# Neighbourhood attention in column blocks of eight, in a one-core transformer kernel

## The chip, the cores and the metric

The kernel runs on one core of a Trainium2 chip, in one launch. The metric is the device time of the whole program in microseconds. It computes two transformer blocks one after the other on 1024 tokens of 1024 channels, all in float32.

## The reference

Only the first block holds neighbourhood attention. 1024 tokens lie on a grid of 16 rows by 64 columns; a query sees 8 rows by 16 columns of keys, clamped inside the grid, with a learned bias over the offset. There are 8 heads of 64 channels.

```python
def neighbourhood_attention(q, k, v, rpb):
    B, S, H, Dh = q.shape
    rows = S // GRID_W
    kh = min(NA_ROWS, rows)
    kw = NA_COLS
    qg = q.reshape(B, rows, GRID_W, H, Dh)
    kg = k.reshape(B, rows, GRID_W, H, Dh)
    vg = v.reshape(B, rows, GRID_W, H, Dh)
    cols = jnp.arange(GRID_W)
    col_start = jnp.clip(cols - kw // 2, 0, GRID_W - kw)
    col_idx = col_start[:, None] + jnp.arange(kw)[None, :]
    col_bias_idx = col_idx - cols[:, None] + (NA_COLS - 1)
    scale = Dh ** -0.5

    def row_block(r):
        row_start = jnp.clip(r - kh // 2, 0, rows - kh)
        q_r = lax.dynamic_index_in_dim(qg, r, axis=1, keepdims=False)
        k_rows = lax.dynamic_slice_in_dim(kg, row_start, kh, axis=1)
        v_rows = lax.dynamic_slice_in_dim(vg, row_start, kh, axis=1)
        k_win = k_rows[:, :, col_idx]
        v_win = v_rows[:, :, col_idx]
        s = jnp.einsum("bqhd,brqchd->bhqrc", q_r, k_win,
                       preferred_element_type=jnp.float32) * scale
        row_bias_idx = row_start + jnp.arange(kh) - r + (NA_ROWS - 1)
        bias = rpb[:, row_bias_idx][:, :, col_bias_idx]
        s = s + jnp.transpose(bias, (0, 2, 1, 3))[None].astype(jnp.float32)
        p = jax.nn.softmax(s, axis=(-2, -1))
        return jnp.einsum("bhqrc,brqchd->bqhd", p.astype(v_win.dtype), v_win)

    out = lax.map(row_block, jnp.arange(rows))
    return jnp.moveaxis(out, 0, 1).reshape(B, S, H * Dh)
```

What stands around it in the block (the second block follows, with another attention and another feed-forward part):

```python
    for l in range(DEPTH):
        h = rms_norm(x, norm1_g[l])
        z = h @ w_in[l]
        a, gate, q, k, v = jnp.split(z, splits, axis=-1)
        conv_out = conformer_conv(a, gate, dw_kernel[l], dw_bias[l],
                                  conv_ln_g[l], conv_ln_b[l])
        q = rms_norm(q.reshape(B, S, N_HEADS, HEAD_DIM), q_norm_g[l])
        k = rms_norm(k.reshape(B, S, N_HEADS, HEAD_DIM), k_norm_g[l])
        v = v.reshape(B, S, N_HEADS, HEAD_DIM)
        attn_out = neighbourhood_attention(q, k, v, rpb[l])
        mix = jnp.concatenate([conv_out, attn_out], axis=-1)
        x = x + mix @ w_out[l]
        h = rms_norm(x, norm2_g[l])
        x = x + (jax.nn.silu(h @ w_gate[l]) * (h @ w_up[l])) @ w_down[l]
```

## The kernel before

**Layout.** Activations lie by channels: a tile is 128 channels by 1024 tokens. A weight unit is 128 x 1024 numbers that SyncE loads (`load_unit`), GpSimd splits into a high and a low part (`split`, L339 and L341) and TensorE multiplies with the high and low parts of the activations in three products (`chunk`, L445), 48 matmuls of 512 columns. Each engine has a hand-written program; semaphores order them. Within an engine the instructions and their waits stand in the order in which they run.

**Ahead of the attention.** Units 0 to 7 give the gated input of the convolution. After each pair ScalarE takes a sigmoid (L916) and VectorE multiplies (L1257). ScalarE also issues the DMAs that build the bias tables in DRAM: 8 DMAs fill them with a masking value (L889), and `bias_windows` lays the bias in with 46 more, 16 large (L904) and 30 small (L911), between its second and third sigmoid. The depthwise convolution has 31 taps for each of 4 channel groups, 124 steps of VectorE (`conv`, L1236), which are spread between its other work.

**The attention.** It runs over four pairs of heads, c = 0 to 3. Each pair has three weight units (q, k, v; units 8 to 19 in all). VectorE evacuates each (L1273), ScalarE and VectorE normalise q and k by head and split them into high and low (`head_hi` L939, `head_lo` L1286). TensorE transposes v (L579) and ScalarE copies it (L955). Then 16 turns follow, n = 0 to 15: head n // 8, row pair n % 8. A turn has the 128 queries of two grid rows and the 8 or 9 key rows that they see (`key_rows`), so 512 or 576 keys of all 64 columns. Half of the turns have 9 rows. A turn goes so:

- TensorE `scores(n)` (L541): three products of q and k; 9 rows need a second matmul of 64 columns each. The result lies in one buffer of two PSUM banks, so `scores(n)` waits for `scores_max` of turn n - 1.
- VectorE adds the bias table and takes the row minimum of the negated sum (L1352). For 9 rows the bias is `bias_inner`, made at the start of each head (L1340 to L1343).
- ScalarE takes the exponential and its sum (L964).
- VectorE takes the reciprocal (L1293) and multiplies the probabilities by it (L1295).
- TensorE `turn(n)` (L556) transposes 4 or 5 blocks, ScalarE copies them (L848, called at L990 and L991), TensorE `values(n)` (L567) multiplies them with v.

TensorE's order is scores(n + 1), values(n - 1), turn(n). ScalarE's is exps(n + 1), the copy of n. VectorE's is bias and minimum of n, one convolution step (c < 3), reciprocal and multiply of n. In c = 3 the convolution is done. The layer norm of its output, its Silu (L977) and the split of the output projection's input (`mix_hi` on ScalarE, `mix_lo` L1264 on VectorE) stand between the turns instead. At the end of a pair ScalarE copies the output (L998).

SyncE loads the table of a head into `bias_table0` or `bias_table1` (L267), 2 DMAs a pair, once the head before is done with the buffer. `BD` in DRAM holds 16 rows of 64 keys for each of 128 queries of a head.

## Time and profile before

| | us |
|---|---|
| Median of 3 runs | 2851.19 |
| Lowest and highest run | 2848.6, 2851.89 |
| Span of the profiled execution | 2856.6 |
| TensorE busy, of the span | 2690.8 (94%) |
| VectorE busy | 1339.3 (47%) |
| ScalarE busy | 680.0 (24%) |
| GpSimd busy | 1009.8 (35%) |

PE is TensorE, DVE VectorE, ACT ScalarE, POOL GpSimd, SP SyncE; a "q" behind the name is the engine's queue, where DMAs are issued. A row of the timeline has the start, the length, the engine, the line, the operation with output and input, and in brackets how long the engine had been idle and what ended it. x8 joins eight instructions into one row. A row for a stretch gives its bounds and length, then for each engine the busy time and the number of instructions, and then the clock that TensorE was granted (1.00 is 2.4 GHz, 0.50 is 1.2 GHz), the DMA share and GB/s. A line number can be that of a helper.

### The profile page before, as it was taken

To read this page: it belongs to the slowest core of one execution; us is meant where nothing else is said; L and a number is where in the kernel's file an instruction comes from. 1 tells how busy PE (TensorE), PEld (TensorE's weight loads), DVE (VectorE), ACT (ScalarE), POOL (GpSimd) and SP (SyncE) were. 2 spreads that over 40 slices of the span, in tenths; PEclk is the share of its full clock that TensorE was granted. 3 is DMA by queue.
4 is the path that set the end of the run, shared out by engine and by line. 5 is a ranking of instruction groups with operands and counts; after the bars stand their busy time and mean duration, and the time that the engine had idled before them with its cause. 6 is when DMAs were issued, how large, how long until landed. Compare 5 with 4: busy or idle time off the path is not lost.

```text
span 2856.6 us, 29102 instructions
## 1 busy us (share of the span) xinstructions
PE 2690.8 (94%) x11492; PEld 2066.8 (72%) x11492; DVE 1339.3 (47%) x1449; ACT 680.0 (24%) x1016; POOL 1009.8 (35%) x554
## 2 busy tenths in 40 slices
PE   8798988899999999999989999997999999999979
PEld 6566766687888888887765665565788888888857
DVE  7768885424222222222755656755622222222465
ACT  3033444412000001000315445531300011100241
POOL 3311012043344444443533333324434343343353
PEclk9869998799999999999999999998999999999989
DMA  5200000121111111111100000001011111111112
GB/s 183 61 15 30 30 30 8 48 71 44 51 47 49 51 44 51 44 51 37 55 30 8 16 23 8 15 23 37 30 52 47 49 51 44 51 44 51 52 37 81
DMA packets 49351, 125.24 MB, mean 44 GB/s; under 512 B 19696, under 2 KB 19696, under 8 KB 48240
## 3 DMA queue, kind: packets, MB, share of 16 engines
q1 hardware_dynamic: 32400, 118.87, 12.6%
q10 hardware_dynamic: 16864, 5.18, 0.8%
q8 instruction: 59, 0.97, 0.1%
q14 instruction: 28, 0.23, 0.0%
HBM read 115.64 MB, written 9.37 MB: 44 GB/s over the span
## 4 chain that ended last, share of the span: by engine, by line
PE 77%; DVE 9%; issue 5%; ACT 3%; POOL 2%; ACTq 2%; DMA 1%; SPq 0%; POOLq 0%; DVEq 0%
PE ps L445 63%; PE ps L567 3%; PE ps L541 2%; PE ps L774 2%; DVE conv_out L1236 2%; PE ps L760 2%; PE ps L744 2%; PE ps L556 1%; PE ps L468 1%; ACTq L904 1%; POOL weight_hi L339 1%; DVE sb_softplus_lo L1533 1%; ACTq L911 1%; POOL weight_lo L341 1%; POOL branch_out L402 1%
## 5 line engine op out<-in xcount | busy, mean ns | idle before, releaser
L339 POOL TENSOR_TENSOR weight_hi<-weight_raw,zero_col 128x1024 fp32r<-128x1024 f32 (+1 forms) x195 | 373.2, 1914 | 1595.9 <-PE ps L445 1486.8
L445 PE MATMUL ps<-input_hi,weight_hi 128*128 128x512 f32 x2048 | 650.4, 399 | 52.9 <-DVE input_lo L1203 35.4
L445 PE MATMUL ps<-input_lo,weight_hi 128*128 128x512 f32 x2176 | 679.2, 394 | 18.5 <-DVE gate_lo L1603 16.7
L445 PE MATMUL ps<-input_hi,weight_lo 128*128 128x512 f32 x2048 | 634.0, 391 | 0.0
L341 POOL TENSOR_TENSOR weight_lo<-weight_raw,weight_hi 128x1024 fp32r<-128x1024 f32 (+1 forms) x195 | 497.3, 2550 | 15.3
L445 PEld LDWEIGHTS ps<-input_hi,weight_hi 128*128 128x128 f32 x2048 | 384.5, 190 | 161.6 <-issue 59.4
L445 PEld LDWEIGHTS ps<-input_lo,weight_hi 128*128 128x128 f32 x2176 | 413.3, 190 | 109.6 <-ACT input_lo L848 13.8
L445 PEld LDWEIGHTS ps<-input_hi,weight_lo 128*128 128x128 f32 x2048 | 387.2, 189 | 81.7
L445 PE MATMUL ps<-hidden_hi,weight_hi 128*128 128x512 f32 x864 | 232.0, 390 | 3.4 <-DVE hidden_lo L1418 3.4
L445 PE MATMUL ps<-hidden_lo,weight_hi 128*128 128x512 f32 x864 | 231.8, 390 | 0.0
L445 PE MATMUL ps<-hidden_hi,weight_lo 128*128 128x512 f32 x864 | 231.8, 390 | 0.0
L445 PEld LDWEIGHTS ps<-hidden_hi,weight_hi 128*128 128x128 f32 x864 | 162.8, 189 | 37.6 <-issue 3.8
L445 PEld LDWEIGHTS ps<-hidden_hi,weight_lo 128*128 128x128 f32 x864 | 162.8, 188 | 33.9
L445 PEld LDWEIGHTS ps<-hidden_lo,weight_hi 128*128 128x128 f32 x864 | 162.8, 188 | 33.9
L1236 DVE SCALAR_TENSOR_TENSOR conv_out<-glu_padded,taps_sb,conv_out 128x1024 f32<-128x1024 f32 x120 | 171.5, 1429 | 2.3
L1024 ACT ACTIVATE work_b<-work_a 128x1024 f32<-128x1024 f32 x32 | 34.0, 1062 | 563.9 <-DVE work_a L1413 563.9
L1427 DVE TENSOR_TENSOR branch_out<-ps,branch_out 128x1024 f32<-128x1024 f32 x56 | 65.9, 1219 | 204.8 <-PE ps L445 204.8
L1427 DVE TENSOR_TENSOR residual<-ps,residual 128x1024 f32<-128x1024 f32 x48 | 56.5, 1218 | 156.1 <-PE ps L445 156.1
L1413 DVE SCALAR_TENSOR_TENSOR work_a<-ps,token_scale 128x1024 f32<-128x1024 f32 x32 | 39.2, 1224 | 177.0 <-PE ps L445 168.0
L1405 DVE TENSOR_TENSOR work_c<-ps,token_scale 128x1024 f32<-128x1024 f32 x22 | 26.9, 1224 | 203.0 <-PE ps L445 203.0
L567 PE MATMUL ps<-probs_t,v_tokens 128*64 128x128 f32 (+1 forms) x576 | 98.1, 320 | 19.4 <-ACT probs_t L848 18.9
L1022 ACT ACTIVATE work_b<-work_a 128x1024 f32<-128x1024 f32 x22 | 23.4, 1062 | 378.5 <-DVE work_a L1402 378.5
(228 smaller groups left out, 2926.1 us busy)
## 6 DMA issues: line engine op xcount, KB each, us to landing
weight_raw<-w_ff SPq DMA_DIRECT2D x40, 512.0 KB, 3.5
weight_raw<-w_mlp SPq DMA_DIRECT2D x32, 512.0 KB, 3.5
weight_raw<-w_mlpd SPq DMA_DIRECT2D x32, 512.0 KB, 3.5
weight_raw<-w_ffd SPq DMA_DIRECT2D x20, 512.0 KB, 3.6
weight_raw<-w_out SPq DMA_DIRECT2D x16, 512.0 KB, 3.5
weight_raw<-w_in SPq DMA_DIRECT2D x16, 512.0 KB, 3.5
residual<-x SPq DMA_DIRECT2D x7, 1024.0 KB, 10.2
weight_raw<-w_qkv SPq DMA_DIRECT2D x12, 512.0 KB, 3.6
```

The source lines that it names most:

```text
L339: pool_.tensor_tensor(WH[:, slot, 0:width], raw, ZERO[:].to_broadcast([P, width]), ALU.add).then_inc(s["w_hi"], 1)
L341: pool_.tensor_tensor(WL[:, slot, 0:width], raw, WH[:, slot, 0:width].bitcast(f32), ALU.subtract).then_inc(s["w_split"], 1)
L445: last = mm(PS[:, b + 2 * c + h, :], w[:, slot, k * n + P * c:k * n + P * (c + 1)], a[:, k, h * H2:(h + 1) * H2], start=(k == 0 and step = ...
L541: last = mm(PS[:, 2 + b, 0:w], q[lo:lo + DH, rp * P:(rp + 1) * P], k_[lo:lo + DH, ks * GRID_W + b * 512:ks * GRID_W + b * 512 + w], start= ...
L567: last = mm(PS[DH * h:DH * (h + 1), 6 + rp // 4, (rp % 4) * P:(rp % 4 + 1) * P], V[0:w, ks // 2 + b, DH * h:DH * (h + 1)], PT[n % 2][0:w, ...
L744: last = mm(PS[:, n % 4, lo:], k_[r:r + DH, b * P:(b + 1) * P], q[r:r + DH, half * H2 + lo:(half + 1) * H2], start=(step == 0), stop=(step ...
L760: mm(PS[:, n % 4, lo:], NONE[:], RUN[n % 2][:, lo:], start=False, stop=False, skip_group_check=True)
L774: mm(PS[DH * h:DH * (h + 1), 6 + half, lo:], V2[:, b, DH * h:DH * (h + 1)], AW[n % 2][:, lo:], start=(b == 4 * half + 3), stop=(b == 0), s ...
L1024: act_.activation(TB[:], TA[:], ACT.Square).then_inc(s["ff_silu"], 1)
L1236: ins = stt(Y[:, c, :], src, TP[:, c, t:t + 1], Y[:, c, :], ALU.mult, ALU.add)
L1413: stt(TA[:], bank(b), 0.0, RS[:], ALU.max, ALU.mult).then_inc(s["bank_free"], 1)
L1427: ins = tt(dst, src, dst, ALU.add)
```

## The change

The queries are tiled by columns. Tokens are stored in 8 column blocks of 8 columns by 16 rows, 128 tokens each (`by_block`, `by_row` are the two views of one tile). A turn has the 128 queries of one block and all 16 rows of the blocks beside it: 3 key blocks, or 2 at the two edges (`key_blocks`). The rows outside the 8 of a query are masked by the bias table. Turns alternate between the two heads (`na_turn`). Scores fit one PSUM bank and there are two buffers of them, and two of the transposed probabilities in PSUM; in SBUF there are three of the scores. TensorE's order becomes scores(n + 2), values(n - 1), turn(n). The multiply by the reciprocal moves from VectorE to ScalarE, ahead of the next exponential. VectorE's order becomes bias and minimum of n + 1, reciprocal of n, the step beside it.

q and k (high and low), v at its evacuation and the output are written from one order into the other, in runs of 8 columns. The DRAM table is 64 x 7 x 120 numbers: one DMA masks it, 55 lay the bias in. GpSimd fills four SBUF tables with the masking value, and SyncE loads each head's table with 16 DMAs of 8 partitions, 32 a pair, 128 in all.

```diff
-def key_rows(rp):
-    first = [min(max(r - NA_ROWS // 2, 0), ROWS - NA_ROWS) for r in (2 * rp, 2 * rp + 1)]
-    return first[0], first[1] + NA_ROWS - first[0]
+CBLOCKS, CBW = 8, 8
+QB = ROWS * CBW
+N_KB = 7
+def na_turn(n):
+    return n % 2, n // 2
+def key_blocks(j):
+    first, last = max(j - 1, 0), min(j + 1, CBLOCKS - 1)
+    return first, last + 1 - first, 3 if j == 0 else 5 if j == CBLOCKS - 1 else 0
+def by_block(t):
+    return t.rearrange("p (b r c) -> p r b c", b=CBLOCKS, c=CBW)
+def by_row(t):
+    return t.rearrange("p (r b c) -> p r b c", b=CBLOCKS, c=CBW)
...
-        BT = [at(f"bias_table{i}", [P, 16, GRID_W], U4 + 4096 * i) for i in range(2)]
-        BI = at("bias_inner", [P, 9, GRID_W], U4 + 8192)
-        SB = [at(f"scores{i}", [P, 9 * GRID_W], U4 + 8192 + 2304 * (i + 1)) for i in range(2)]
-        ST = at("softmax_stats", [P, 3, 16], U4 + 8192 + 3 * 2304)
+        BT = [at(f"bias_table{i}", [P, N_KB, QB], U4 + 4 * N_KB * QB * i) for i in range(4)]
         OC = [at(f"attn_out{c}", [P, T], up32(c * UW)) for c in range(4)]
         QH, QL, KH, KL = (at(n, [P, T], QK0 + 4096 * i, f32r)
                           for i, n in enumerate(("q_hi", "q_lo", "k_hi", "k_lo")))
         V = at("v_tokens", [P, 8, P], QK0 + 16384)
-        PT = [at(f"probs_t{i}", [P, 5, P], QK0 + 20480 + 2560 * i) for i in range(2)]
+        PT = [at(f"probs_t{i}", [P, 3, P], QK0 + 20480 + 1536 * i) for i in range(2)]
+        SB = [at(f"scores{i}", [P, 3 * QB], QK0 + 23552 + 1536 * i) for i in range(3)]
+        ST = at("softmax_stats", [P, 3, 16], QK0 + 28160)
...
-        BD = nc.dram_tensor("bias_tables", [HEADS, P, 16 * GRID_W], f32).ap()
-        N_TABLE_DMAS = 2 * (HEADS + NA_COLS - 1)
+        BD = nc.dram_tensor("bias_rows", [HEADS * CBW, N_KB, (2 * NA_ROWS - 1) * CBW], f32).ap()
+        N_TABLE_DMAS = N_KB * CBW - 1
...
-                for h in (2 * c, 2 * c + 1):
-                    if h >= 2:
-                        sp.wait_ge(s["scores_max"], 8 * (h - 1))
-                    sp.wait_ge(s["scale_ready"], 1)
+                if c == 0:
+                    sp.wait_ge(s["bt_masked"], 4)
                     sp.wait_ge(s["table_out"], 16 * N_TABLE_DMAS)
-                    sp.dma_start(BT[h % 2][:], BD[h]).then_inc(s[f"bt_in{h % 2}"], 16)
+                elif c >= 2:
+                    sp.wait_ge(s["scores_max"], 16 * (c - 1))
+                for i in range(2):
+                    h, buf = 2 * c + i, 2 * (c % 2) + i
+                    for r in range(ROWS):
+                        first = min(max(r - NA_ROWS // 2, 0), ROWS - NA_ROWS)
+                        b0 = first - r + NA_ROWS - 1
+                        sp.dma_start(BT[buf][r * CBW:(r + 1) * CBW, :, first * CBW:(first + NA_ROWS) * CBW],
+                                     BD[h * CBW:(h + 1) * CBW, :, b0 * CBW:(b0 + NA_ROWS) * CBW])\
+                            .then_inc(s[f"bt_in{buf}"], 16)
...
-            splits(2, U_TAIL + 2 * TAIL - 2)
+            splits(2, 2)
+            pool.wait_ge(s["scale_ready"], 1)
+            for i in range(4):
+                pool_.memset(BT[i][:], MASKED).then_inc(s["bt_masked"], 1)
+            splits(4, U_TAIL + 2 * TAIL - 4)
...
-                    h, rp = n // 8, n % 8
-                    ks, nk = key_rows(rp)
+                    h, j = na_turn(n)
+                    kb, nb, _ = key_blocks(j)
                     lo = DH * h
                     if n == 0:
                         pe.wait_ge(s["qk_hi"], 2 * c + 2)
                         pe.wait_ge(s["qk_lo"], 2 * c + 2)
-                    else:
-                        pe.wait_ge(s["scores_max"], 16 * c + n)
+                    elif n >= 2:
+                        pe.wait_ge(s["scores_max"], 16 * c + n - 1)
                     for q, k_, step in ((QH, KH, 0), (QH, KL, 1), (QL, KH, 2)):
-                        for b, w in ((0, 512), (1, nk * GRID_W - 512)):
-                            if w:
-                                last = mm(PS[:, 2 + b, 0:w], q[lo:lo + DH, rp * P:(rp + 1) * P],
-                                          k_[lo:lo + DH, ks * GRID_W + b * 512:ks * GRID_W + b * 512 + w],
-                                          start=(step == 0), stop=(step == 2))
+                        last = mm(PS[:, 2 + n % 2, 0:nb * QB], q[lo:lo + DH, j * QB:(j + 1) * QB],
+                                  k_[lo:lo + DH, kb * QB:(kb + nb) * QB],
+                                  start=(step == 0), stop=(step == 2))
                     last.then_inc(s["scores_done"], 1)
                 def turn(n):
-                    _, nk = key_rows(n % 8)
                     pe.wait_ge(s["probs_scaled"], 16 * c + n + 1)
-                    if n:
-                        pe.wait_ge(s["pt_sb"], 16 * c + n)
-                    else:
+                    if n >= 2:
+                        pe.wait_ge(s["pt_sb"], 16 * c + n - 1)
+                    elif n == 0:
                         pe.wait_ge(s["v_ready"], c + 1)
-                    for b in range(5 if nk == 9 else 4):
-                        w = P if b < 4 else GRID_W
-                        last = nc.tensor.transpose(PS[0:w, 4 + b // 4, (b % 4) * P:(b % 4 + 1) * P],
-                                                   SB[n % 2][:, b * P:b * P + w], IDENT[:])
+                    for b in range(key_blocks(na_turn(n)[1])[1]):
+                        last = nc.tensor.transpose(PS[:, 4 + n % 2, b * P:(b + 1) * P],
+                                                   SB[n % 3][:, b * QB:(b + 1) * QB], IDENT[:])
                     last.then_inc(s["pt_done"], 1)
                 def values(n):
-                    h, rp = n // 8, n % 8
-                    ks, nk = key_rows(rp)
+                    h, j = na_turn(n)
+                    kb, nb, _ = key_blocks(j)
                     pe.wait_ge(s["pt_sb"], 16 * c + n + 1)
-                    nb = 5 if nk == 9 else 4
                     for b in range(nb):
-                        w = P if b < 4 else GRID_W
-                        last = mm(PS[DH * h:DH * (h + 1), 6 + rp // 4, (rp % 4) * P:(rp % 4 + 1) * P],
-                                  V[0:w, ks // 2 + b, DH * h:DH * (h + 1)], PT[n % 2][0:w, b, :],
+                        last = mm(PS[DH * h:DH * (h + 1), 6 + j // 4, (j % 4) * P:(j % 4 + 1) * P],
+                                  V[:, kb + b, DH * h:DH * (h + 1)], PT[n % 2][:, b, :],
                                   start=(b == 0), stop=(b == nb - 1), skip_group_check=True)
                     last.then_inc(s["pv_done"], 1)
...
+                scores(1)
                 for n in range(16):
-                    if n < 15:
-                        scores(n + 1)
+                    if n < 14:
+                        scores(n + 2)
...
-            for h in range(HEADS):
-                act.dma_start(BD[h], NEG[:]).then_inc(s["neg_out"], 16)
+            act.dma_start(BD.rearrange("q k b -> q (k b)"), NEG[0:HEADS * CBW, 0:N_KB * 15 * CBW]).then_inc(s["neg_out"], 16)
             def bias_windows():
-                act.wait_ge(s["neg_out"], 16 * HEADS)
+                act.wait_ge(s["neg_out"], 16)
                 rows, cols = 2 * NA_ROWS - 1, 2 * NA_COLS - 1
+                per = N_KB * rows * CBW
+                def window(q, block, x0, x1, bias_col):
+                    dst = bass.AP(tensor=BD.tensor, offset=q * per + block * rows * CBW + x0,
+                                  ap=[[CBW * per, HEADS], [CBW, rows], [1, x1 - x0]])
+                    src = bass.AP(tensor=rpb.tensor, offset=bias_col,
+                                  ap=[[rows * cols, HEADS], [cols, rows], [1, x1 - x0]])
+                    act.dma_start(dst, src).then_inc(s["table_out"], 16)
                 half = NA_COLS // 2
-                inner = GRID_W - NA_COLS + 1
-                with nc.allow_non_contiguous_dma(reason="64-byte windows of the bias"):
...
+                with nc.allow_non_contiguous_dma(reason="windows of the bias, 32 bytes at most"):
+                    for q in range(CBW):
+                        window(q, 0, q, CBW, half - 1)
+                        window(q, 1, 0, CBW, 2 * half - 1 - q)
+                        if q:
+                            window(q, 2, 0, q, 3 * half - 1 - q)
+                        for k in range(2):
+                            window(q, 3 + k, 0, CBW, NA_COLS - 1 - q + CBW * k)
+                            window(q, 5 + k, 0, CBW, half - 1 - q + CBW * k)
...
-                    copy((QH, KH)[j][:], (TA, TB)[j][:]).then_inc(s["qk_hi"], 1)
+                    copy(by_block((QH, KH)[j][:]), by_row((TA, TB)[j][:])).then_inc(s["qk_hi"], 1)
...
+                    act.wait_ge(s["probs_sum"], 16 * c + n + 1)
+                    act_.activation(SB[n % 3][:, 0:w], SB[n % 3][:, 0:w], ACT.Identity,
+                                    scale=ST[:, 2, n:n + 1]).then_inc(s["probs_scaled"], 1)
...
-                copy(OC[c][:], bank(6)).then_inc(s["attn_out_done"], 1)
-            act.wait_ge(s["attn_out_done"], 4)
+                for half in range(2):
+                    copy(by_row(OC[c][:]).rearrange("p r b c -> p b r c")[:, 4 * half:4 * half + 4],
+                         PS[:, 6 + half, :].rearrange("p (b r c) -> p b r c", b=4, c=CBW))\
+                        .then_inc(s["attn_out_done"], 1)
...
-                    tt(t[:], bank(2 * ((u + j) % 2)), RS[:], ALU.mult).then_inc(s["bank_free"], 1)
+                    if j < 2:
+                        tt(t[:], bank(2 * ((u + j) % 2)), RS[:], ALU.mult).then_inc(s["bank_free"], 1)
+                    else:
+                        tt(by_block(t[:]), by_row(bank(2 * ((u + j) % 2))), by_row(RS[:]), ALU.mult)\
+                            .then_inc(s["bank_free"], 1)
...
-                    tt((QL, KL)[j][:], (TA, TB)[j][:], (QH, KH)[j][:].bitcast(f32), ALU.subtract)\
-                        .then_inc(s["qk_lo"], 1)
+                    tt(by_block((QL, KL)[j][:]), by_row((TA, TB)[j][:]), by_block((QH, KH)[j][:].bitcast(f32)),
+                       ALU.subtract).then_inc(s["qk_lo"], 1)
+                def scores_in(m):
+                    h, j = na_turn(m)
+                    _, nb, at_bias = key_blocks(j)
+                    w, buf = nb * QB, 2 * (c % 2) + h
+                    if j == 0:
+                        dve.wait_ge(s[f"bt_in{buf}"], 16 * ROWS * (c // 2 + 1))
+                    dve.wait_ge(s["scores_done"], 16 * c + m + 1)
+                    if m >= 3:
+                        dve.wait_ge(s["pt_done"], 16 * c + m - 2)
+                    dve_.tensor_tensor_reduce(
+                        out=SB[m % 3][:, 0:w], in0=PS[:, 2 + m % 2, 0:w],
+                        in1=BT[buf][:, at_bias:at_bias + nb, :].rearrange("p b k -> p (b k)"),
+                        scale=-1.0, scalar=3.0e38, op0=ALU.add, op1=ALU.min,
+                        accum_out=ST[:, 0, m:m + 1]).then_inc(s["scores_max"], 1)
                 def probs(m):
-                    w = key_rows(m % 8)[1] * GRID_W
                     dve.wait_ge(s["probs_done"], 16 * c + m + 1)
-                    chain(dve_.reciprocal(ST[:, 2, m:m + 1], ST[:, 1, m:m + 1]))
-                    chain.wait()
-                    ts(SB[m % 2][:, 0:w], SB[m % 2][:, 0:w], ST[:, 2, m:m + 1], None, ALU.mult)\
-                        .then_inc(s["probs_scaled"], 1)
+                    dve_.reciprocal(ST[:, 2, m:m + 1], ST[:, 1, m:m + 1]).then_inc(s["probs_sum"], 1)
                 if c == 3:
@@ -1330,29 +1382,11 @@
                 dve.wait_ge(s["qk_scaled"], 2 * c + 2)
                 head_lo(1)
                 evac(2, TC)
+                scores_in(0)
                 for n in range(16):
...
-                        chain(dve_.tensor_copy(BI[:], BT[h % 2][:, 3:12, :]))
-                        chain(dve_.memset(BI[0:GRID_W, 8, :], MASKED))
-                        chain(dve_.memset(BI[GRID_W:P, 0, :], MASKED))
...
+                    if n < 15:
+                        scores_in(n + 1)
+                    probs(n)
```

## Rows read from the trace of the kernel before

**Rows 1.** Stretches, the turn loops of c=0, 1, 3; last: clock, DMA share, GB/s.
```profile
167.60:236.20 68.60, 66.20 (x297) 47.52 (x297) 46.95 (x89) 24.98 (x57) 1.00 (x1) 0.68 0.07 24
...
279.70:332.30 52.60, 48.86 (x297) 35.42 (x297) 47.29 (x89) 24.72 (x57) 3.15 (x2) 0.97 0.09 31
...
475.30:558.30 83.00, 67.89 (x301) 47.36 (x301) 38.59 (x84) 43.32 (x76) 0.00 (x0) 0.73 0.00 0
```

**Rows 2.** Timeline: start, length (us), engine, line; VectorE in a turn of c=1.
```profile
300.17 0.69 DVE L1352 CUSTOM_DVE_ANT_0 scores<-ps,bias_table 128x512 f32<-128x512 f32 x1 [0.24 <-PE ps L541]
...
300.79 1.28 DVE L1236 SCALAR_TENSOR_TENSOR conv_out<-glu_padded,taps_sb,conv_out 128x1024 f32<-128x1024 f32 x1
...
302.10 0.16 DVE L1293 RECIPROCAL softmax_stats<-softmax_stats 128x1 f32<-128x1 f32 x1
...
302.30 0.48 DVE L1295 TENSOR_SCALAR scores<-scores,softmax_stats 128x512 f32<-128x512 f32 x1
...
303.16 0.69 DVE L1352 CUSTOM_DVE_ANT_0 scores<-ps,bias_table 128x512 f32<-128x512 f32 x1 [0.37 <-PE ps L541]
```

**Rows 3.** Timeline, TensorE in two turns of 8 key rows of c=0.
```profile
207.13 0.79 PE L541 MATMUL ps<-k_hi,q_hi 64*128 64x512 f32 x1
...
208.70 1.97 PE L567 MATMUL ps<-probs_t,v_tokens 128*64 128x128 f32 x8
...
210.60 1.12 PE L556 MATMUL ps<-identity,scores 128*128 128x128 f32 x4
211.65 0.50 PE L541 MATMUL ps<-k_hi,q_hi 64*128 64x512 f32 x1
...
214.14 0.50 PE L541 MATMUL ps<-k_hi,q_hi 64*128 64x512 f32 x1
```

**Rows 4.** Timeline, TensorE at the start of two turns of 9 key rows, c=0.
```profile
184.99 0.85 PE L541 MATMUL ps<-k_hi,q_hi 64*128 64x512 f32 x2
...
190.82 0.79 PE L541 MATMUL ps<-k_hi,q_hi 64*128 64x512 f32 x1
```

**Rows 5.** A stretch of 3 us in turns of 9 key rows, c=0.
```profile
197.00:200.00 3.00, 3.00 (x11) 2.04 (x10) 1.67 (x3) 1.32 (x4) 0.00 (x0) 0.50 0.00 0
```

**Rows 6.** Groups by form, 160 to 560 us: busy us, mean ns, idle before.
```profile
L848 ACT ACTIVATE probs_t<-ps 128x512 f32<-128x512 f32 x64 | 37.4, 584 | 20.7 <-PE ps L556 20.7
...
L1352 DVE CUSTOM_DVE_ANT_0 scores<-ps,bias_inner 128x576 f32<-128x576 f32 x32 | 24.2, 755 | 17.8 <-PE ps L541 17.0
...
L964 ACT ACTIVATE scores<-scores,softmax_stats 128x512 f32<-128x512 f32 x32 | 23.1, 721 | 38.7 <-DVE softmax_stats L1352 38.7
```

**Rows 7.** Timeline, ScalarE and VectorE late in c=3.
```profile
529.15 4.63 ACT L977 ACTIVATE conv_out<-conv_out,gains_sb 128x1024 f32<-128x1024 f32 x4
...
552.32 1.23 DVE L1264 TENSOR_TENSOR input_lo<-attn_out,input_hi 128x1024 fp32r<-128x1024 f32 x1 [1.83 <-ACT input_hi L848]
```

**Rows 8.** Timeline ahead of the loops; line L911 alone (ns: least, median, most).
```profile
39.08 9.02 ACTq L889 DMA_DIRECT2D bias_tables<-masked_tile  x8
...
L911 ACTq DMA_DIRECT2D bias_tables<-rpb x30: 648/648/3467, 67.3 to 104.9; - x30
...
94.01 11.49 ACTq L911 DMA_DIRECT2D bias_tables<-rpb  x15
...
105.55 1.06 ACT L916 ACTIVATE work_b<-work_a 128x1024 f32<-128x1024 f32 x1 [51.12 <-issue]
...
106.72 2.37 DVE L1257 TENSOR_TENSOR glu_padded<-work_c,work_b 128x1024 f32<-128x1024 f32 x1 [14.93 <-ACT work_b L916]
...
137.90 3.78 PE L468 MATMUL ps<-squares,mean_head 128*128 128x512 f32 x4 [19.39 <-ACT squares L932]
```

**Rows 9.** Line L267 alone; ScalarE's timeline: a table load, a later identity.
```profile
L267 SPq DMA_DIRECT2D bias_table<-bias_tables x8: 326/326/377, 107.1 to 422.9; - x8
...
535.59 1.28 ACT L964 ACT_TABLE_LOAD   x1
...
646.83 2.19 ACT L873 ACTIVATE input_hi<-residual,gains_sb 128x1024 fp32r<-128x1024 f32 x2 [8.56 <-PE ps L445]
```

55 lines of the change are left out of this document (11 added, 44 removed).

## The prediction

> **What bounds the kernel now.** I read the page first, then the chain of waits, then the stretches, then single turns in the timeline. The page's chain puts most of the span on matmuls of the weight units, which the change leaves alone; what it touches lies between 42 us and 581 us. There the same pattern comes four times, once for each pair of heads c: three weight units (q, k, v), and then 16 attention turns. The stretches [rows 1] give the turns' length: 68.6 us for c=0, 52.6 for c=1 (c=2 is the same, 52.5), 83.0 for c=3, together 256.7 us. The reader should see the granted clock beside them: 0.68 and 0.73 in the long ones, 0.97 in the short ones.
>
> At c=1 and c=2 one turn takes VectorE 2.99 us (the scores of one turn at 300.17, of the next at 303.16), of which 0.37 us is waiting for the scores from TensorE [rows 2]. So VectorE and TensorE bound it together, since there is one score buffer. At c=0 TensorE bounds it alone: at half clock a turn of 8 key rows takes it 4.52 us (207.13 to 211.65), at full clock 2.49 us (211.65 to 214.14) [rows 3], and a turn of 9 key rows at half clock 5.83 us (184.99 to 190.82) [rows 4]. The stretch 197 to 200 shows TensorE busy all of the time, at a clock of 0.50 [rows 5]. Being busy did not bring the clock back there.
>
> **A turn after the change.** 12 of the 16 turns of a pair have three key blocks (384 columns), 4 have two (256), in place of 512 or 576.
>
> VectorE: the bias-and-minimum goes from 512 to 384 columns. Its slope, from 689 and 755 ns at 512 and 576 [rows 2, 6], is 1.03 ns a column, so it holds the engine 0.62 - 0.13 = 0.49 us. The convolution step stays (1.31 us from start to start), the reciprocal too (0.20), and the multiply at L1295 (0.49 us) goes [rows 2]. Sum 2.00 us, 1.87 with two blocks; 16 turns are 31.5 us. The copy of `bias_inner` and its memsets go as well; they are part of the 52.6 us.
>
> ScalarE takes the multiply over. Exp costs 721 ns at 512 columns and the copy of the transposed probabilities 584 [rows 6]; at 384 columns, with some 0.12 us of overlap, I take 0.5 for exp, 0.19 for reading its sum, 0.5 for the new scaling, 0.45 for the copy: 1.7 us. That hides beside VectorE's 2.0 and beside TensorE, and costs nothing while either is slower.
>
> TensorE: at half clock, the 8-row turn splits into scores 1.57 us, values 1.90, transposes 1.05 [rows 3]. Two 512-column scores start 0.43 us apart there, so 128 columns are 0.107 us, and three score matmuls of 384 take 1.57 - 3 x 0.107 = 1.25. Values and transposes go from four blocks to three: 1.43 and 0.79. Sum **3.47 us**; with two blocks 2.41. Sixteen turns are 51.3 us. At full clock the same shares of 2.49 us give 1.9 us, just under VectorE's 2.00. So the clock decides: 2.0 or 3.5 us a turn. With a start of some 5 us and a tail of 1 to 2 us, a pair costs 37 us or 54 us.
>
> **Which clock.** I compare how much of a turn is columns streaming, at 0.107 us for 128 columns and twice that for each matmul of a value or transpose block (8 and 4 of them in an 8-row turn). The 8-row turn then streams 3 x 0.43 + 12 x 0.213 = 3.84 us of its 4.52, or 0.85; the 9-row turn (64 columns more, 15 matmuls) 4.64 of 5.83, or 0.80. At 0.50 clock the 9-row turns stayed at half clock; in both long stretches the clock rose within 8-row turns. The new turn (3 x 0.32 + 9 x 0.213) streams 2.88 us of 3.47, or 0.83, and with its small overheads taken in full (3.56 us) 0.81. That is nearer to the turns that did not recover. And the start of each pair, where TensorE waits for q, k and the first softmax, is unchanged, and the clock was at half at the start of all four loops, for about 3 us at c=1 and c=2. So I take half clock for most of each loop.
>
> The Trainium skill, "TensorE: Matmul & The Clock Gate", section "Why this matters for your kernels", advises to keep TensorE busy without a break to reach full clock. The stretch with busy 3.00 of 3.00 at 0.50 [rows 5] disagrees. By the page's rule the new loops would all run fast; that is the rival below.
>
> **The four loops, at half clock.** Three scores lie ahead of the first transposes (0.93 + 0.93 + 1.25 = 3.1 us), so what follows the start is 51.3 - 3.1 = 48.2.
> - c=0: start 5.3 (6.1 before; exp and scale now have two blocks), 48.2, tail 1.0: 54.5 for 68.6, gain 14.
> - c=1, c=2: 4.5 (5.1 before) + 48.2 + 1.0, less 2 for turns that still run at full clock: 51.7 for 52.6, gain 1 each. What VectorE saves there is not on the path, since TensorE is late instead. The next unit needs no convolution that isn't done.
> - c=3: layer norm and output split lie between the turns. Up to its first transposes 8.2 (7.4 before, and one score more); the first three turns, of which two carry a table load, Ln and Exp of the layer norm on ScalarE (2.6 each), 10.3; seven turns at 3.47, 24.3; the turn in which four Silus hold ScalarE for 4.63 us [rows 7], with their table load and a copy 7.0, 10.5; one turn with the table load of 1.28 us, 4.1; four turns 12.5; tail 1.5. Sum 71.4 for 83.0, gain 11.6. In its last turns the bound was a ring of waits: VectorE waited 1.83 us for ScalarE's copy [rows 7] before it took the reciprocal. The new order takes the reciprocal first and opens the ring; next late is TensorE (3.47) or ScalarE (1.7 and its copy of 1.0).
>
> **In front of the loops.** ScalarE issues the bias tables' DMAs from 54.4 to 105.5 us, and the sigmoid behind them waits 51.12 us; VectorE waits 14.93 us for that sigmoid; at 137.90 TensorE has been idle 19.39 us [rows 8]. So this queue sets the end here. Eight writes of the mask table become one (9.02 us of issue from 39.08 on [rows 8], less one of 1.2), so the first sigmoid comes before VectorE needs it, and the windows start about 3 us earlier. 46 windows become 55, all of the small kind at L911, median 648 ns, at worst 3467 [rows 8]. One group of 15 took 11.49 us, 0.77 each [rows 8], and behind the large windows others took up to 0.87. At 0.65 the 55 end at 87, at 0.87 at 99. VectorE can't be at the sigmoid's result before 89. Gain 6 to 17, taken **12**, all on the path: unit 8's result was there at 118.5 (137.90 less 19.39), some 17 us before VectorE came for it, so up to 17 us nothing else is late.
>
> Moved past SP: 128 table loads of 56 pieces each take the place of 8. One load held SP 0.33 us [rows 9]; 32 at 0.33 to 1.6 us are 10 to 52 us, from 99 at the latest, and the first scores need them at about 155 (167.6 less 12). The loads for c=1 to c=3 and the weights behind them have the length of a loop. Cost 0; from 1.8 us a load on the scores would wait, and a load with 0.33 is far from it. GpSimd fills four tables ahead of its split of unit 4; TensorE is then at work on units 2 and 3 (11 us each), and the split waits for that: cost 0, at worst a few us.
>
> **Layout.** q, k (high and low), v and the output are written in chunks of 8 columns: about 6.8 us a pair of 1.0 to 1.2 us instructions. The trace shows none with such chunks. The nearest rows are the same instructions without chunks, so I take no difference; doubled they would cost 27 us in all. Less than nothing is excluded: no element falls away.
>
> Sum: 12 + 14 + 1 + 1 + 11.6 = **40 us**. The profiled execution spans 2856.6, the median of the runs is 2851.2, so 5 less: 2817 in a profile, **2811** in the runs.
>
> **The rivals.**
> 1. *Full clock in one or both of c=1 and c=2.* These two regained it in 3 us before (0.97 in their rows). Then each gains 16 instead of 1 (start and tail 5, and 31.5, for 52.6). Time 2796 or 2781. Against it: the new turn's share. Chance 0.22.
> 2. *Full clock everywhere.* c=0 gains 30, c=3 25: 12 + 30 + 16 + 16 + 25 = 99 us, 2752. For it: TensorE no longer waits within a turn. Chance 0.15.
> 3. *Chunked layout or slow table loads* take 15 to 40 us back: 2826 to 2851. Chance 0.08.
> 4. *Slower: the new scaling needs another function table than exp.* Then each turn loads twice, 2 x 1.28 = 2.57 us, on ScalarE: 1.7 + 2.6 = 4.3 us a turn, 275 us in 64 turns, with starts and c=3's extras 308 for 256.7. Less 12 in front: 2890. It decides from a turn of 3.7 us on. Against it: the same function ran at 646.83 under the table that was loaded for exp at 535.59, with no load between [rows 9]. Chance 0.05, with other losses of that size in it. The Trainium skill, "ScalarE: Activation LUTs", section "Table sets: the hidden batching unit", says that identity is in every set; rows 9 agree.
>
> My forecast has the other 0.50; its own range, from the front's bounds and 3.47 or 3.56 a turn, is 2800 to 2825.
>
> **Numbers.** A difference under 0.2% (6 us) can't be told from none. Faster: 0.50 + 0.22 + 0.15 + most of 0.08 = 0.93; same 0.02; slower 0.05. The range takes in rival 2 and half of rival 3: 2748 to 2836.
>
> **What would show it.** In the new profile: scores, values and transposes at 3.5 us a turn with a clock near 0.5 in the four loops, or 2.0 us with 1.0; VectorE's turn without L1295; the sigmoid's wait near 38 us; TensorE's 19.4 us gap near 7; no table loads beyond the present ones; the loops at 54, 52, 52 and 71 us. Wrong it is if the clock rises in three-block turns, or if a strided write takes more than 1.3 us.

## The result and the profile after

| | before | after |
|---|---|---|
| Median of the runs | 2849.89 us (4 runs, 2848.35 to 2851.89) | 2831.70 us (4 runs, 2830.00 to 2833.28) |
| Span of the profiled execution | 2856.6 us | 2828.3 us |
| VectorE busy | 1339.3 us | 1288.7 us |
| ScalarE busy | 680.0 us | 682.7 us |
| GpSimd busy | 1009.8 us | 1014.6 us |

The ratio is 0.9933, with a 95% interval from 0.9919 to 0.9948. The change makes the kernel faster by 18.2 us, where the forecast said 40. The sign was right and the time lies in the range, but the gain is less than half of the forecast one.

The stretches of the changed kernel, from the first score of each loop of turns to its last value, and what lies between them. After the bounds and the length come the busy times of TensorE, its weight load, VectorE, ScalarE and GpSimd, then the granted clock. They answer to [rows 1].

```profile
156.56:213.53 56.97, 54.37 (x189) 37.25 (x189) 32.57 (x67) 25.38 (x65) 2.92 (x2) 0.50 0.06 15
213.53:259.25 45.72, 40.50 (x153) 30.69 (x153) 36.53 (x34) 12.95 (x16) 10.60 (x5) 0.91 0.12 30
259.25:313.36 54.11, 50.84 (x189) 34.81 (x189) 32.58 (x67) 25.41 (x65) 3.02 (x2) 0.56 0.05 13
313.36:358.70 45.34, 40.13 (x153) 30.25 (x153) 37.80 (x35) 12.95 (x16) 10.60 (x5) 0.92 0.12 30
358.70:413.15 54.45, 51.19 (x189) 35.13 (x189) 32.58 (x67) 25.41 (x65) 3.01 (x2) 0.56 0.05 13
413.15:461.56 48.41, 39.83 (x158) 30.16 (x157) 29.70 (x27) 17.18 (x20) 14.54 (x6) 0.92 0.04 11
461.56:527.28 65.72, 56.44 (x193) 37.62 (x193) 25.48 (x62) 44.05 (x84) 0.00 (x0) 0.53 0.00 1
```

The reader should see the clock column. All four loops run at half clock almost throughout, also those of c=1 and c=2, which had 0.97 in [rows 1]. The work of a turn shrank, VectorE fell from 47.3 to 32.6 us a loop, and the loops of c=1 and c=2 are still 1.5 and 2 us longer than they were.

One turn of c=0 on VectorE (start, length, engine, line, operation; in brackets the idle time before it and what ended it). It answers to [rows 2]:

```profile
173.43 0.56 DVE L1339 CUSTOM_DVE_ANT_0 scores<-ps,bias_table 128x384 f32<-128x384 f32 x1 [1.73 <-PE ps L571]
173.92 0.08 DVE L1339 DVE_READ_ACCUMULATOR2_ANT softmax_stats<- 128x1 f32 x1
173.92 0.16 DVE L1348 RECIPROCAL softmax_stats<-softmax_stats 128x1 f32<-128x1 f32 x1
173.99 1.26 DVE L1270 SCALAR_TENSOR_TENSOR conv_out<-glu_padded,taps_sb,conv_out 128x1024 f32<-128x1024 f32 x1
177.00 0.56 DVE L1339 CUSTOM_DVE_ANT_0 scores<-ps,bias_table 128x384 f32<-128x384 f32 x1 [1.74 <-PE ps L571]
```

The turn is 3.57 us here, of which VectorE waits 1.74 for TensorE. The multiply is gone.

In front of the loops: ScalarE's queue, its sigmoid, VectorE behind it, and TensorE's gap. They answer to [rows 8]:

```profile
51.82 38.19 ACTq L931 DMA_DIRECT2D bias_rows<-rpb  x55
90.06 1.06 ACT L946 ACTIVATE work_b<-work_a 128x1024 f32<-128x1024 f32 x1 [37.18 <-issue]
91.23 1.22 DVE L1291 TENSOR_TENSOR glu_padded<-work_c,work_b 128x1024 f32<-128x1024 f32 x1 [0.42 <-ACT work_b L946]
129.81 3.44 PE L500 MATMUL ps<-squares,mean_head 128*128 128x512 f32 x4 [9.93 <-ACT squares L962]
```

The 55 windows took 0.69 us each. The sigmoid waits 37.18 us for them instead of 51.12, VectorE 0.42 instead of 14.93, and TensorE's gap is 9.93 instead of 19.39. The loops start at 156.56 instead of 167.59 [rows 1].

### The profile page after: what moved, and what is told of

Its sections match the earlier page's. It is cut to its first block, busy times and chain, and to the rows that moved or that the text cites. A ratio compares the mean times of both kernels' runs of the same rounds, so it can differ in the third digit from the quotient of the medians.

```text
span 2828.3 us, 28250 instructions
## 1 busy us (share of the span) xinstructions
PE 2680.4 (95%) x11060; PEld 2053.4 (73%) x11060; DVE 1288.7 (46%) x1361; ACT 682.7 (24%) x1052; POOL 1014.6 (36%) x558
## 4 chain that ended last, share of the span: by engine, by line
PE 78%; DVE 10%; issue 5%; ACT 3%; POOL 2%; ACTq 1%; DMA 0%; SPq 0%; POOLq 0%; DVEq 0%
PE ps L477 64%; PE ps L593 3%; DVE conv_out L1270 2%; PE ps L571 2%; PE ps L802 2%; PE ps L584 2%; PE ps L788 2%; PE ps L772 2%; ACTq L931 1%; DVE sb_softplus_lo L1566 1%; PE ps L500 1%; POOL weight_hi L367 1%; POOL weight_lo L369 1%; POOL branch_out L434 1%; PE ps L792 1%
## 5 line engine op out<-in xcount | busy, mean ns | idle before, releaser
L477 PE MATMUL ps<-input_lo,weight_hi 128*128 128x512 f32 x2176 | 684.0, 396 | 19.1 <-DVE gate_lo L1636 17.3
L1270 DVE SCALAR_TENSOR_TENSOR conv_out<-glu_padded,taps_sb,conv_out 128x1024 f32<-128x1024 f32 x120 | 178.9, 1491 | 2.4
L593 PE MATMUL ps<-probs_t,v_tokens 128*64 128x128 f32 x352 | 90.7, 427 | 12.8 <-ACT probs_t L876 12.8
```

Source lines behind the costliest of these rows:

```text
L477: last = mm(PS[:, b + 2 * c + h, :], w[:, slot, k * n + P * c:k * n + P * (c + 1)], a[:, k, h * H2:(h + 1) * H2], start=(k == 0 and step = ...
L593: last = mm(PS[DH * h:DH * (h + 1), 6 + j // 4, (j % 4) * P:(j % 4 + 1) * P], V[:, kb + b, DH * h:DH * (h + 1)], PT[n % 2][:, b, :], start ...
L1270: ins = stt(Y[:, c, :], src, TP[:, c, t:t + 1], Y[:, c, :], ALU.mult, ALU.add)
```

## The experiments

**The theory.** At half clock the new turn takes TensorE 3.56 us, where a turn of 8 rows took 4.52 and one of 9 rows 5.83 [rows 3, 4], but the loops now stay at half clock, and that is where the gain stays. What decides is not how much of a turn is streaming, by which my forecast chose, but the entry of a loop: the clock is lost there, and the new turns neither lose nor regain it. **The rivals** are that the mix of matmuls within a turn decides the clock (the forecast's own reason), that something else than the clock bounds the new loops (the chunked layout, the tables, ScalarE), and that part of the missing gain is no loss at all but comes from the profile that the sum started from.

### The base of the sum

The kernel before was run again, unchanged, ten times.

> The kernel before, unchanged, timed and profiled again. Its profile before spanned 2856.6 us, while its four runs had a median of 2849.9; the profiled run of the changed kernel spans 2828.3 with a median of 2831.7. Theory A (the clock of the loop at c=0 differs from one execution to the next, and the profile of before was one where it rose late): the span here is 2845 to 2852 us, and the loop of c=0 is some 3 to 9 us shorter than 68.6 us, the other loops the same. Rival B (the profile adds its own cost to the kernel before): the span is again 2856 and the loop at c=0 68.6.

Measured: 2851.32 us, a ratio of 1.0003 (0.9993 to 1.0013), with runs from 2847.24 to 2857.80. This time the profiled execution spans 2846.6 us, 10.0 less than the one that the forecast read. Its stretches:

```profile
167.76:224.55 56.79, 54.27 (x297) 39.43 (x297) 46.77 (x89) 24.71 (x57) 1.03 (x1) 0.85 0.08 29
224.55:267.82 43.27, 38.05 (x153) 28.86 (x153) 36.62 (x35) 12.89 (x15) 10.60 (x5) 0.96 0.08 25
267.82:323.51 55.69, 52.73 (x297) 38.31 (x297) 47.38 (x89) 24.71 (x57) 3.11 (x2) 0.88 0.09 29
...
366.76:422.47 55.71, 52.69 (x297) 38.27 (x297) 47.39 (x89) 24.71 (x57) 3.12 (x2) 0.88 0.09 29
...
469.48:546.36 76.88, 64.52 (x301) 45.67 (x301) 38.67 (x84) 43.23 (x76) 0.00 (x0) 0.74 0.00 1
```

The same program gives c=0 56.8 us here and 68.6 in [rows 1], c=1 55.7 and 52.6, c=3 76.9 and 83.0. The start is the same (167.76 and 167.59). So in the kernel before each loop's length hangs on when the clock rises in it, and this differs from execution to execution. TensorE's transposes show when, at c=0:

```profile
178.90 1.12 PE L556 MATMUL ps<-identity,scores 128*128 128x128 f32 x4
183.90 1.14 PE L556 MATMUL ps<-identity,scores 128*128 128x128 f32 x5
187.47 0.77 PE L556 MATMUL ps<-identity,scores 128*128 128x128 f32 x5
```

The second row belongs to turn 2, the first with 9 rows. Its five transposes would take 1.33 us at half clock and take 0.77 at full, so the clock rose in the middle of them. At c=1 and c=2 it rose in turn 2 as well (five in 1.15 us at c=1), and at c=3 in turn 5, all of them turns of 9 rows. In the profile that the forecast read, the loop of c=0 stayed at half through all its 9-row turns of the first head and rose only behind them.

Against this execution the change gives 11.2 us in front, -0.2 at c=0, 1.6 and 1.3 at c=1 and c=2, 11.2 at c=3, and loses 5.9 in the three stretches between. The spans differ by 18.3 us, as the medians do (18.2). This is theory A, only wider: it had 3 to 9 us at c=0 and the other loops unchanged. Rival B, a cost of the profiling, falls, since this profiled run took 2848.53 us among runs of 2847.24 to 2857.80.

### Is it the clock?

Extra matmuls whose results nobody reads were put into the loops of the changed kernel: twelve ahead of turn 0, and four in each of turns 1 to 3 of c=0 to c=2.

```diff
+                def warm(b, count):
+                    for _ in range(count):
+                        mm(PS[:, b, :], QH[:, 0:P], KH[:, 0:512], start=True, stop=True)
...
                     if n < 14:
                         scores(n + 2)
+                    if n == 0:
+                        warm(5, 12)
+                    elif n < 4 and c < 3:
+                        warm(0, 4)
                     if n:
                         values(n - 1)
                     turn(n)
```

> The changed kernel with filler matmuls (128x512, into a bank that nobody reads): 12 ahead of the first transposes of each pair, 4 in each of turns 1 to 3 for c=0 to 2. Nothing else differs. Theory A (the clock decides the turn: 3.56 us at half, about 2.0 at full, where VectorE is the bound): the clock is up from the third turn on in c=0 to c=2 and stays up, each of these loops falls from 54 to 57 us to 38 to 41 us, and the run is 40 to 50 us faster than the changed kernel, near 2785 us. Rival B (the chain of waits from exp over reciprocal, scaling, transposes and copy bounds the turn too): the clock rises but a turn stays above 2.6 us, and the gain is under 25 us. Rival C (the clock falls again in the turns without fillers): gain under 10 us.

Measured: 2781.59 us (2781.00 to 2782.51), a ratio of 0.9748 (0.9732 to 0.9764), so more work gives 50 us less than the changed kernel, as theory A had it. The loops of c=0 to c=2 take 41.6, 38.65 and 38.64 us at clocks of 0.92, 1.00 and 1.00. VectorE in two turns of c=0:

```profile
178.92 1.27 DVE L1278 SCALAR_TENSOR_TENSOR conv_out<-glu_padded,taps_sb,conv_out 128x1024 f32<-128x1024 f32 x1
180.22 0.56 DVE L1347 CUSTOM_DVE_ANT_0 scores<-ps,bias_table 128x384 f32<-128x384 f32 x1
180.71 0.08 DVE L1347 DVE_READ_ACCUMULATOR2_ANT softmax_stats<- 128x1 f32 x1
180.84 0.17 DVE L1356 RECIPROCAL softmax_stats<-softmax_stats 128x1 f32<-128x1 f32 x1
180.92 1.27 DVE L1278 SCALAR_TENSOR_TENSOR conv_out<-glu_padded,taps_sb,conv_out 128x1024 f32<-128x1024 f32 x1
```

From one step to the next (178.92 to 180.92) it is 2.00 us, the forecast's number for full clock, and VectorE has no idle time left. The chunked layout, the tables and ScalarE are the same in this kernel, so the rival that one of them bounds the loops falls.

Then the extra matmuls were spread: c + 1 of them in every turn, and none at the entry beyond that.

> The changed kernel with fillers in every turn, of the same kind: 1 a turn at c=0, 2 at c=1, 3 at c=2, none at c=3. At half clock one costs TensorE 0.43 us. Theory A (how densely columns stream through a turn is what lets the clock rise or keeps it down): at c=0 the clock stays at half through the loop (turns of 4.0 us, loop near 62 us), at c=2 it rises and the loop is near 40 us, c=1 lies on one or the other side. Rival B (the clock is down because of the pauses at the start of the pair, not of the turns): all three stay at half, with turns of 4.0, 4.4 and 4.8 us.

Measured: 2814.74 us in one run.

```profile
158.68:223.22 64.54, 63.32 (x205) 40.74 (x205) 30.68 (x66) 25.36 (x65) 1.02 (x1) 0.53 0.05 12
267.45:309.97 42.52, 40.98 (x221) 26.20 (x221) 31.32 (x66) 25.48 (x65) 3.03 (x2) 1.00 0.07 17
353.56:399.25 45.69, 44.49 (x237) 29.19 (x237) 31.51 (x66) 25.39 (x65) 3.04 (x2) 1.00 0.06 16
```

One wide matmul in each turn left c=0 at half clock and cost 7.6 us there. Two and three a turn held full clock at c=1 and c=2, which come in at it. That is the pattern of theory A, but it doesn't show theory A, since two and three matmuls also shorten the wait ahead of turn 0. Against the 34.6 us that these loops reach further below, 8 and 11 us are the price of the matmuls themselves.

The same matmuls as in the first of these kernels, in the kernel before:

> The kernel before with the fillers of e1_warm_start: 12 ahead of the first transposes of each pair, 4 in each of turns 1 to 3 for c=0 to 2. Theory A (the clock was also what made the loop of c=0 long before, and c=1 and c=2 had it at full already): the loop at c=0 falls from 60 to 68 us to about 53, c=1 and c=2 stay within 2 us of 52.6, the run is 8 to 16 us faster than the kernel before, near 2837. Then the retiling itself, both at full clock, is worth about 50 us. Rival B: no change within 0.2%.

Measured: 2853.57 us (2851.41 to 2859.95), a ratio of 1.0002 (0.9991 to 1.0013). Two of its loops:

```profile
169.14:228.45 59.31, 57.81 (x321) 41.62 (x321) 46.77 (x89) 24.83 (x57) 1.03 (x1) 0.91 0.08 27
271.98:326.95 54.97, 53.33 (x321) 38.51 (x321) 47.43 (x89) 24.83 (x57) 3.13 (x2) 1.00 0.09 29
```

The clock rose here too, to 1.00 at c=1, and nothing was gained; the 8 to 16 us that theory A expected did not come. At full clock VectorE works on an old turn for all but 0.24 to 0.37 of its 2.99 us [rows 2], so an old loop at full clock has little left to gain from a faster TensorE. The clock is not worth nothing to them: c=0 took 68.6 us at 0.68 and 56.8 at 0.85. But they regain most of it by themselves, and the 24 extra matmuls of a loop cost about as much as they bring: c=1 takes 55.0 us at 1.00 with them and took 52.6 at 0.97 without. With the same extra matmuls in both kernels, the change is worth 72.0 us (2853.57 less 2781.59) in place of 18.2.

### Where the clock is lost

The entries of c=0 (first row) and of c=1 in the changed kernel, TensorE:

```profile
156.56 0.51 PE L571 MATMUL ps<-k_hi,q_hi 64*128 64x256 f32 x1 [2.16 <-DVE work_c L1310]
...
259.25 0.38 PE L571 MATMUL ps<-k_hi,q_hi 64*128 64x256 f32 x1 [1.32 <-DVE work_c L1310]
...
263.23 0.44 PE L584 MATMUL ps<-identity,scores 128*128 128x128 f32 x2 [1.61 <-ACT scores L1000]
...
265.46 0.44 PE L571 MATMUL ps<-k_hi,q_hi 64*128 64x384 f32 x1
265.74 0.37 PE L571 MATMUL ps<-k_lo,q_hi 64*128 64x384 f32 x1
265.91 0.52 PE L571 MATMUL ps<-k_hi,q_lo 64*128 64x384 f32 x1
266.36 1.11 PE L593 MATMUL ps<-probs_t,v_tokens 128*64 128x128 f32 x4
```

TensorE waits 1.61 us for the first softmax, does one turn at full clock, and is at half clock from about 265.8 on: the four value matmuls that took 0.65 us take 1.11. From 266 to 300 it is busy 34.00 of 34.00 us, and the clock is 0.50 all the time. At c=0 the loop comes in at half clock already: the clock was 1.00 until 156.5, and fell at the end of a wait of 2.16 us.

In the kernel before, the same happens at c=1:

```profile
284.79 0.66 PE L556 MATMUL ps<-identity,scores 128*128 128x128 f32 x4 [1.96 <-DVE scores L1295]
...
286.72 1.95 PE L567 MATMUL ps<-probs_t,v_tokens 128*64 128x128 f32 x8
```

Up to the 1.96 us wait and just behind it the clock is full (four transposes in 0.66 us), then the eight value matmuls take 1.95 us, as at half clock (1.97 in [rows 3]).

The next kernel has the twelve matmuls ahead of turn 0 of c=0 to c=2, which close this wait, and none in the turns.

```diff
                     if n < 14:
                         scores(n + 2)
+                    if n == 0 and c < 3:
+                        warm(5, 12)
                     if n:
                         values(n - 1)
                     turn(n)
```

> The changed kernel with the twelve extra 128x512 matmuls ahead of the first transposes of the turn loops of c=0 to c=2, and without the four in each of turns 1 to 3. (Their results are never read.) With both, the loops took 41.6, 38.7 and 38.6 us at a clock of 0.92, 1.00 and 1.00 and the kernel 2781.6 us. Theory A, the clock is settled by how TensorE enters the loop: the loops are 36 to 40 us each and the time is 2781.6 less three times twelve matmuls of 0.22 us, 2773 to 2779 us. Theory B, entering at full clock is not enough, since in the changed kernel the loops of c=1 and c=2 were entered at full clock and fell two or three turns in: the waits of turns 1 to 3 lose it again, c=1 and c=2 take 54 to 57 us each, c=0 40 to 60, and the time is 2815 to 2840 us.

Measured: 2769.71 us (2768.79 to 2772.21), ratio 0.9718 (0.9702 to 0.9734), 3 us below theory A's window of 2773 to 2779.

```profile
158.43:196.53 38.10, 36.50 (x201) 25.90 (x201) 31.29 (x66) 25.29 (x65) 1.02 (x1) 0.92 0.08 21
196.53:240.06 43.53, 38.31 (x153) 29.06 (x153) 38.59 (x35) 12.96 (x16) 10.60 (x5) 0.96 0.12 31
240.06:275.16 35.10, 33.50 (x200) 23.68 (x200) 31.13 (x66) 25.29 (x65) 3.04 (x2) 1.00 0.08 21
```

The turns are the changed kernel's own, and they hold full clock to the end of the loop. So their mix of matmuls does not lose it; the entry does. The wait of 1.32 us ahead of the first score of c=1 is still there (240.06), and the clock did not fall behind it alone. Whether it is the length of the second wait that counts, or both waits together, nothing here separates; closing the second is enough. The second row shows one thing more: the stretch behind the loop is 43.53 us instead of 45.72, since its first weight unit starts at full clock.

Five matmuls in place of the twelve:

> The kernel with extra matmuls ahead of turn 0 of c=0 to c=2, but five instead of twelve: 1.1 us at full clock, under the 1.61 us that TensorE waited there in c=1 of the changed kernel. Theory A, the wait ahead of turn 0 is what loses the clock, and most of it filled is enough at c=1 and c=2: their loops take 33.5 to 35 us; c=0, which comes in at half clock (12 filled 4.1 us and raised it), stays at 0.50 and 55 to 58 us: time 2782 to 2788 us. Theory B, the length of the run matters: all three loops fall back to 54 to 57 us, 2828 to 2835 us. Theory C, any filling will do: all three at 33 to 37 us, 2764 to 2769 us.

Measured: 2766.03 us (2765.79 to 2768.87), theory C. The loops take 36.39, 34.60 and 34.60 us at 0.91, 1.00 and 1.00. Even c=0, which comes in at half clock, rises with 2.4 us of wide matmuls. I had expected it to need more. The stretches behind the loops of c=0 and c=1 take 44.65 and 44.28 us, about 1 us more than with twelve. The trace shows where at c=0: TensorE waits 3.90 us for ScalarE in the middle of the stretch in both kernels, and the clock falls there in both, but with five it falls before the four 512-column matmuls behind the wait (3.78 us), with twelve during them (3.06 us).

Twenty narrow matmuls (128 columns each), with as many columns as five wide ones:

> The changed kernel with twenty extra matmuls of 128 columns ahead of turn 0 of c=0 to c=2, in place of the five or twelve of 512 columns: as many columns as five wide ones, 1.1 us of them at full clock, more with what each costs beside its columns. Theory A, what counts is that TensorE has no gap ahead of turn 0, whatever the matmuls: c=1 and c=2 keep full clock (34 to 37 us each), and c=0, which comes in at half, rises as with five wide ones (36 to 39 us): 2765 to 2775 us. Theory B, narrow matmuls close the gap but cannot raise the clock: c=1 and c=2 34 to 37 us, c=0 at 0.50 and 56 to 60 us: 2786 to 2794 us. Theory C, narrow ones neither hold nor raise it: all at 54 us or more, 2832 us or more.

Measured: 2791.22 us (2789.72 to 2793.34), theory B.

```profile
157.14:217.32 60.18, 58.65 (x209) 41.61 (x209) 32.58 (x67) 25.28 (x65) 1.03 (x1) 0.50 0.05 13
...
262.91:297.57 34.66, 33.06 (x209) 23.74 (x209) 30.85 (x66) 25.53 (x65) 3.03 (x2) 1.00 0.08 21
```

These two rows separate two things. A loop that comes in at full clock (c=1) keeps it as soon as the wait is closed, with matmuls of either width. A loop that comes in at half clock (c=0) stays there: narrow matmuls ran 4.53 us without a gap ahead of turn 0 and did not raise it, and the loop stays at 0.50 for all of its 60 us. Five wide ones did.

Five wide matmuls in turn 4, in the middle of the loop, where there is no wait to close, and none at the entry:

> The changed kernel with five extra matmuls of 512 columns in turn 4 of the loops of c=0 to c=2 only, where TensorE is busy without a gap at half clock; nothing ahead of turn 0. Theory A, a run of wide matmuls raises the clock anywhere and the turns then hold it: from turn 5 on turns of 2.00 us, the loops of c=0 to c=2 take 40 to 46 us each, the time is 2790 to 2805 us. Theory B, only the gap ahead of turn 0 counts, and once the loop runs at half clock it stays: the loops are as in the changed kernel plus five matmuls (2 us each), 2834 to 2842 us.

Measured: four runs of 2824.80, 2799.21, 2781.67 and 2800.24 us. The runs lie in steps of some 20 us. The profiled execution is the longest; its loops take 43.21, 58.21 and 56.89 us. At c=0 the clock rose:

```profile
174.99 2.50 PE L562 MATMUL ps<-k_hi,q_hi 128*128 128x512 f32 x5
177.42 1.32 PE L597 MATMUL ps<-probs_t,v_tokens 128*64 128x128 f32 x6
178.68 0.55 PE L588 MATMUL ps<-identity,scores 128*128 128x128 f32 x3
```

The transposes after it take 0.55 us for three, where they took 0.90, and the turns are 2.0 us to the end. At c=1 and c=2 the same five did not raise it. So wide matmuls can raise the clock in mid-loop, and the turns then hold it, but these five did so only once of three times in this execution, and by the step between the runs (18 to 25 us for each loop that rises) twice in two of the others and three times in the fourth. The granted clock of the runs, averaged over the whole program, steps the same way: 0.946 here, 0.956 in the runs of about 2800 us, 0.964 in that of 2781.67. In which loops it rose there was not seen. Neither theory had this.

### What the second score buffer is worth

TensorE's order goes back to that of the kernel before, so that only one score buffer is in use at a time; first without extra matmuls.

```diff
-                    elif n >= 2:
-                        pe.wait_ge(s["scores_max"], 16 * c + n - 1)
+                    else:
+                        pe.wait_ge(s["scores_max"], 16 * c + n)
...
-                scores(1)
                 for n in range(16):
-                    if n < 14:
-                        scores(n + 2)
+                    if n < 15:
+                        scores(n + 1)
```

> The changed kernel with that same older order of the scores and nothing else: one score buffer in use at a time, no extra matmuls. Theory A, at half clock TensorE has 2.4 us of transposes and value matmuls between the scores of one turn and those of the next, which hides VectorE's read: turns stay at 3.56 us, the loops within 1 us each and the time 2828 to 2836 us. Theory B, the second buffer carries the gain of the change: turns grow by 0.5 us or more, 2850 us or more.

Measured: 2845.35 us (2841.07 to 2847.59), between the two theories: 13.7 us slower than the changed kernel. Its loops take 59.3, 58.0, 57.4 and 69.1 us, 2.3 to 3.9 more each. A three-block turn at half clock is 3.64 us instead of 3.56, and turns 1 and 2 wait 0.34 and 0.43 us for ScalarE. Theory A had TensorE's own work as the bound, which it is, but not these small waits, which add up over 64 turns and four starts. At c=1 the clock falls sooner too: behind the wait of 1.80 us ahead of turn 0 TensorE is at half clock at once, where the changed kernel still does one turn at full clock.

The same order together with the twelve matmuls ahead of turn 0:

> The kernel with twelve extra matmuls ahead of turn 0 (2769.7 us, turns of 2.00 us at full clock), with the order of the kernel before: the scores of turn n+1 are issued in turn n and wait until VectorE has read those of turn n, so one score buffer is in use at a time. Theory A, the second buffer is what lets a full-clock turn run without a gap: the turn becomes 2.3 to 3.0 us, the loops of c=0 to c=2 take 40 to 48 us and the time is 2782 to 2808 us; if the gaps also lose the clock, up to 2825 us. Theory B, the second buffer hides nothing: within 3 us of 2769.7 us.

Measured: 2844.93 us (2843.58 to 2847.57), 75 us slower than with two buffers, and past the end of either theory. The entry of c=1, TensorE:

```profile
265.36 3.02 PE L562 MATMUL ps<-k_hi,q_hi 128*128 128x512 f32 x12
...
270.70 0.44 PE L588 MATMUL ps<-identity,scores 128*128 128x128 f32 x2 [0.80 <-ACT scores L1005]
...
273.33 0.90 PE L588 MATMUL ps<-identity,scores 128*128 128x128 f32 x3 [0.90 <-ACT scores L1005]
```

The loop enters at full clock, then TensorE waits 0.80 and 0.90 us for the scaled probabilities in turns 1 and 2, and the clock is at half from there on; the loops take 60.1, 57.4 and 57.4 us. So the second buffer is worth 14 us to the changed kernel. With the wait ahead of turn 0 closed, it decides whether there is a full clock at all: it takes away the two waits behind which the clock falls.

### Where the multiply stands

The scaling back on VectorE, behind the reciprocal, in the changed kernel:

```diff
-                    act.wait_ge(s["probs_sum"], 16 * c + n + 1)
-                    act_.activation(SB[n % 3][:, 0:w], SB[n % 3][:, 0:w], ACT.Identity,
-                                    scale=ST[:, 2, n:n + 1]).then_inc(s["probs_scaled"], 1)
...
-                    dve_.reciprocal(ST[:, 2, m:m + 1], ST[:, 1, m:m + 1]).then_inc(s["probs_sum"], 1)
+                    chain(dve_.reciprocal(ST[:, 2, m:m + 1], ST[:, 1, m:m + 1]))
+                    chain.wait()
+                    ts(SB[m % 3][:, 0:w], SB[m % 3][:, 0:w], ST[:, 2, m:m + 1], None, ALU.mult)\
+                        .then_inc(s["probs_scaled"], 1)
```

> The changed kernel with one part undone: the scaling of the probabilities is back on VectorE behind the reciprocal, and ScalarE's Identity is gone. In the changed kernel a turn takes 3.56 us at half clock and VectorE waits 1.74 us of it for TensorE. Theory A, TensorE at half clock hides either place: loops as in the changed kernel within 1 us, time 2828 to 2834 us. Theory B, the multiply behind the 1.27 us step of the convolution on VectorE lengthens the chain from scores to transposes past what the second score buffer covers: each turn grows by 0.3 us or more, time 2845 us or more.

Measured: 2828.92 us (2827.42 to 2830.06), theory A and 2.8 us less than the changed kernel. At c=3 ScalarE is busy 36.43 us instead of 44.05, and the loop takes 63.44 instead of 65.72. At half clock this part of the change brought nothing, and took some 2.3 us where ScalarE is loaded.

The same with the extra matmuls of the first kernel of this kind:

> The kernel with the extra matmuls at the start of each loop (2781.6 us), and the scaling of the probabilities moved from ScalarE back to VectorE behind the reciprocal. At full clock a three-block turn of c=0 to c=2 took 2.00 us with VectorE at work without a gap. Theory A, VectorE is the bound at full clock, as the forecast had it (2.00 us a turn): the multiply on 384 columns, some 0.5 us by the 0.755 us that it took on 576, comes on top, the loops of c=0 to c=2 grow from 38.6 to 43 to 47 us and the time is 2795 to 2808 us. Theory B, TensorE is the bound at 1.99 us and VectorE only keeps step: VectorE has room elsewhere, the loops grow by under 2 us each and the time is 2781 to 2788 us.

Measured: 2787.15 us (2785.76 to 2789.49), 5.6 more than with the multiply on ScalarE. That is theory B's window, and the loops grew by under 2 us, as theory B had it. But its reason does not hold: VectorE has no idle time in a turn that went from 2.00 to 2.33 us (one step at 179.46, the next at 181.78), so VectorE sets its length. The loops of c=1 and c=2 grew from 38.65 to 40.3 only, because without the move the four extra matmuls make each of turns 1 to 3 some 2.9 to 3.1 us long and leave VectorE slack there. The stretches behind c=0 and c=1 grew as well, from 43.5 to 45.3 and 45.2, and c=3 is 2.6 us shorter: 1.7 + 1.6 + 1.7 + 1.8 + 1.6 - 2.6 = 5.8, beside 5.6 between the times. So theory A has the right bound, and its sum is too large; the move gains only at full clock.

### The loop of c=3

Four extra matmuls in every turn of c=3 beside those of the first such kernel:

> The kernel with twelve extra matmuls ahead of turn 0 and four in turns 1 to 3, and in the loop of c=3 four extra matmuls of 128x512 in every turn from 1 to 15, into the bank that the turn's own transposes will overwrite. Before, that loop took 67.6 us at a clock of 0.58. Theory A, the clock bounds that loop too: it rises to 0.95 or more, the loop becomes ScalarE's (44 us busy, with its Silu stall of some 4 us) and takes 50 to 57 us, the kernel 2765 to 2772 us, the fastest so far. Theory B, that loop waits for its own side work on ScalarE and VectorE whatever the clock: the clock rises, the loop stays at 62 us or more, the kernel at 2776 to 2784 us.

Measured: 2774.97 us (2771.76 to 2777.97), between the theories. The loop took 63.06 us at a clock of 0.90. Its middle turns are 3.12 us instead of 2.00, since the extra matmuls are on the path there. So only the gaps were filled, where TensorE waits for ScalarE's table loads (9 and 10 matmuls, turns 2 and 3) and for its Silu (25, turn 11), with twelve ahead of turn 0 and none in the other turns:

> The kernel with twelve extra matmuls ahead of turn 0 in the loops of c=0 to c=2 (2769.7 us), and in the loop of c=3 the twelve ahead of turn 0 too, with 9, 10 and 25 extra matmuls where TensorE waits for ScalarE there (turns 2 and 3 behind the ln/exp table loads, turn 11 behind the Silu), and none in the other turns. The loop took 66.0 us at a clock of 0.53 without, and 63.1 us at 0.90 with four extra in every turn, which made its middle turns 3.12 us instead of 2.00. Theory A, only the gaps have to be filled: clock 0.95 or more, middle turns 2.0 us, the loop 51 to 56 us and the time 2755 to 2762 us. Theory B, in that loop the middle turns do not hold the clock on their own: it falls behind turn 3 and the loop stays at 62 to 70 us, the time 2766 to 2774 us.

Measured: 2759.74 us (2758.77 to 2760.70), ratio 0.9681 (0.9659 to 0.9702), in theory A's window. The loop takes 56.71 us at a clock of 0.86, both a little short of what theory A asked for (51 to 56 us, 0.95); the clock falls to half clock behind a wait of 1.95 us at turn 12. With that one filled too (9, 3, 3 and 2 in turns 12 to 15), and five instead of twelve at c=0 to c=2:

> Five wide extra matmuls ahead of turn 0 in c=0 to c=2 (loops of 36.4, 34.6 and 34.6 us), and in c=3 those of the kernel that filled its gaps (loop of 56.7 us, clock 0.86) with 9, 3, 3 and 2 more in turns 12 to 15, where it fell back to half clock behind a wait of 1.95 us. Expected if the gap rule holds: c=3 at 51 to 55 us and a clock above 0.93, the time 2759.7 less 1.7 + 2 x 0.6 for the starts and 2 to 5 for c=3, so 2751 to 2756 us. If the last turns lose it anyway: 2756 to 2760 us.

Measured: **2753.33 us** (2751.74 to 2755.16), ratio 0.9657 (0.9637 to 0.9677), as expected, the fastest version here and 78 us under the changed kernel. The loop of c=3 lies in its range of 51 to 55 us too.

```profile
398.43:451.83 53.40, 51.89 (x266) 36.60 (x266) 25.09 (x61) 43.52 (x84) 0.00 (x0) 0.97 0.00 1
```

## Why the prediction was right and wrong, by its steps

The forecast was 40 us and 18.2 came. By its own terms: 1.0 less in front, 2.3 less at c=0, 5.5 less at c=1 and c=2 together, 5.7 more at c=3, 5.4 lost in the stretches between the loops and 2.8 behind them, which were both put at nothing without a reason, and 10 for the base. **The step that failed first is the base:** the loop lengths of one execution of the kernel before were taken for those of its runs. The second, smaller one is the weight unit behind a loop, which was left out. c=3 came out better than its sum, and hid part of both.

- **In front, 12: measured 11.0** against [rows 1], 11.2 against the second execution. The steps held one by one: 55 DMAs at 0.69 us (0.65 to 0.87 expected), the sigmoid's wait 37.18 (38), TensorE's gap 9.93 (7). The 32 loads of a pair took 22.05 us on SP, 0.69 each, and no score waited for them.
- **VectorE's turn, 2.00: measured 2.00** at full clock. **ScalarE's 1.7** lay beside it: the scaling took 0.61 us and the table was not loaded anew. That excludes rival 4.
- **TensorE's turn, 3.47: measured 3.56.** I had named 3.56 as the value with the overheads taken in full, and took the lower one. That is 0.09 us for each of twelve turns, 1.1 us a loop. At full clock I had 1.9 us, and it is 2.0.
- **The loops of c=0 to c=2, 54.5, 51.7 and 51.7: measured 57.0, 54.1 and 54.4.** The turn's length gives 1.1 of the 2.4 to 2.7 us. The last three value groups wait 0.58, 0.47 and 0.47 us for ScalarE's copy, 1.5 us where the tail had 1.0. The rest, about 0.9, I can't put to a row.
- **c=3, 71.4: measured 65.7.** Up to the third turn it is right (18.3 us for 18.5), and the seven turns took 24.9 for 24.3. The turn with the Silus took 7.97 us instead of 10.5, and the last four turns with the tail 10.7 instead of 14.0: I had counted them at the full 3.1 us, but the last ones have two blocks, and no scores are issued in them.
- **Missing: the weight unit behind a loop.** It begins at the clock at which the loop ends. In the changed kernel its first matmuls of 512 columns ran at half clock until 217.9, and the three stretches between the loops take 2.2, 1.8 and 1.4 us more than in the profile before. With full-clock loops this stretch is back at 43.5. This term of 5.4 us was not in the sum.
- **The base of the sum, "5 less": about 10 too much gain.** This is the largest error. The loop of c=0 with 68.6 us at 0.68 was one draw; the same kernel gave 56.8 in the next profile. The runs' median lies between the two executions (spans of 2846.6 and 2856.6, with 1.9 us around the first). Of the forecast 14 us at c=0, 11.7 came in against the one execution and -0.2 against the other. I took one fixed offset for both kernels, when the spread of the loops was the thing to ask about: the clock rises in them at another time in each execution.

The sum against its own base: 11.0 + 11.7 - 1.5 - 2.0 + 17.3 in front and in the loops is 36.5, less 5.4 between the loops and 2.8 spread behind them, is 28.3, the difference of the spans. Less the 10 of the base this is the 18.2 of the runs.

**The half clock was right, its reason only in part.** The forecast named the entry and said that the new turns do not regain the clock, and both came out. But it misread the entry: the clock was not at half from the start at c=1, it was full until 286.7, fell behind the wait of 1.96 us and was back at 290.2. And it chose between the levels by the share of streaming in a turn. That criterion fails twice. The turns with the same share hold full clock for a whole loop once the wait at the entry is closed. And the rule was read off one profile, in which the 9-row turns of c=0 stayed at half clock; in the second profile of the same kernel the clock rose in a 9-row turn in all four loops. The reading was thin besides: of the new turn's 0.83 and 0.81 the first lies nearer to the 0.85 of the 8-row turns than to the 0.80 of the 9-row ones. So that the level came out right was partly luck.

Why the old loops regained the clock and the new ones do not stays open. The old ones have scores of 512 columns, and the new ones no matmul of more than 384. That the width makes this difference is shown only for the extra matmuls (five of 512 columns raise the clock, twenty of 128 do not), and these contract over 128 partitions, the scores over 64. Scores of 384 against 512 columns were not tried by themselves.

The rule of the Trainium skill, "TensorE: Matmul & The Clock Gate", section "Why this matters for your kernels", that a TensorE kept busy reaches full clock, agrees with the rows where the clock had not been lost, and with the wide matmuls. It does not with the 34.00 busy us of 34.00 at 0.50 at c=1, nor with the narrow ones.

## What to carry to other kernels

Ask of each short wait on TensorE whether the clock is lost in it, and what comes behind it: closing a wait of 1.6 us took 19 us off a loop, since the small matmuls behind it did not win the clock back. A few wide matmuls with no reader, put where TensorE waits anyway, closed it at some 0.2 us each. Before summing gains stage by stage, profile the kernel before twice: a stage whose clock differs between executions is no base for a sum, and a change that takes work out of a stage is worth only what the clock leaves of it.

## What the runs showed of the hardware

- TensorE at half clock, busy with matmuls of 128 to 384 columns for 54.4 of 57.0 us, stayed at 0.50 all the time (c=0 of the changed kernel), and so it did for 58.7 of 60.2 us with twenty narrow ones more. At c=1 it was busy 34.00 of 34.00 us at 0.50.
- In the weight unit behind it the clock rose after 4.4 us of matmuls of 512 columns (213.5 to 217.9); five of them in a row, 2.4 to 2.5 us, raised it at the entry of c=0, and in mid-loop in some executions only.
- In the kernel before, at half clock with scores of 512 columns, the clock rose at c=0 after 44 us of the loop in one execution and after 17 us in the other.
- At full clock, waits of 1.61 us ahead of turn 0, and of 0.80 and 0.90 us in two successive turns, were followed by the fall. In the kernel with twelve matmuls at the entry, a wait of 1.32 us ahead of the first score of c=1 and three of 0.5 us at the end of a loop were not.
- A chunked write in runs of 8 columns took no longer than the same write without chunks: 1.22 us for the evacuation of v, 1.06 for the high parts of q and k, 1.47 for the low part of q, in both kernels. The output is now copied by two instructions of 0.60 us, where one took 1.03.
